# A two-layer diffusion-transformer step on one core: the opening of layer 0 loaded and multiplied in halves of the features, and the first local modulation group moved from steps 3 and 4 to steps 1 and 3

## The reference, cut to what matters

```python
def modulate(cvec, w_mod_l, b_mod_l):
    m = jnp.einsum('bd,de->be', jax.nn.silu(cvec), w_mod_l) + b_mod_l
    return jnp.split(m[:, None, :], N_MOD, axis=-1)

def latent_layer(x, c, ...):
    sh1, sc1, g1, sh2, sc2, g2 = modulate(c, w_mod_l, b_mod_l)
    h = rmsnorm(x, norm1_l) * (1 + sc1) + sh1
    q_mla, ckv, kpe, q_swa, k_swa, v_swa, q_na, k_na, v_na = mixer_projections(h, w_in_l, ...)
    ...
    o_mla = dense_attention(...)
    o_swa = window_attention(...)
    o_na = neighbourhood_attention(..., rpb_l, HEAD_SCALE)
    heads_out = jnp.concatenate([o_mla, o_swa, o_na], axis=-1)
    return residual_tail(x, heads_out, g1, sh2, sc2, g2, ...)
```

## Time and profile before

| What | Value |
|---|---|
| Median of three runs (lowest, highest) | 1337.96 us (1335.44, 1338.13) |
| Profiled execution, its own time | 1338.34 us |
| Its span, first to last instruction | 1336.3 us |
| PE busy / PEld busy | 1279.6 us (96%) / 735.3 us (55%) |
| DVE / ACT / POOL busy | 613.7 / 358.8 / 152.5 us |
| Mean granted TensorE clock | 0.991 of full speed |
| DMA | 313.16 MB, mean 234 GB/s |

### The profile page before, as it was taken

The page is one execution under the profiler, slowest core; times in us unless marked ns, Lnnn a source line. Parts: engine busy times, 40 slices in busy tenths (PEclk is TensorE's granted clock), DMA queues, the critical chain, the costliest instruction groups (busy, mean ns, idle before and its releaser), DMA issues. The chain is left out here.

```text
span 1336.3 us, 17216 instructions
## 1 busy us (share of the span) xinstructions
PE 1279.6 (96%) x6042; PEld 735.3 (55%) x6042; DVE 613.7 (46%) x1519; ACT 358.8 (27%) x931; POOL 152.5 (11%) x257
## 2 busy tenths in 40 slices
PE   6999999999999999999999999989999999999997
PEld 3555555565666564444455555566666656444443
DVE  0132266444566463433343224655556536344438
ACT  1121255434343210000012114563444311100001
POOL 2210220000000110000142003000000011000014
PEclk9999999998999999999999999999899999999999
DMA  9976996499111489999694038430201139999966
GB/s 355 363 248 220 347 332 254 162 359 327 42 64 64 168 333 398 361 374 367 260 334 161 16 140 291 151 128 15 88 33 64 63 130 352 404 368 360 362 270 246
DMA packets 125441, 313.16 MB, mean 234 GB/s; under 512 B 9882, under 2 KB 58426, under 8 KB 112688
## 3 DMA queue, kind: packets, MB, share of 16 engines
q1 hardware_dynamic: 90896, 243.13, 49.8%
q0 software_dynamic: 12848, 45.39, 9.0%
q10 hardware_dynamic: 21616, 23.60, 5.3%
HBM read 232.14 MB, written 80.71 MB: 234 GB/s over the span
## 5 line engine op out<-in xcount | busy, mean ns | idle before, releaser
L790 PE MATMUL ps<-ring,big 128*128 128x384 f32 (+2 forms) x640 | 230.7, 520 | 1.7 <-DVE big L1773 1.3
L790 PEld LDWEIGHTS ps<-ring,big 128*128 128x128 f32 x640 | 120.3, 190 | 104.6 <-issue 63.7
L871 PE MATMUL ps<-ring,arena 128*128 128x512 f32 x384 | 169.3, 594 | 1.9 <-ACT arena L1406 1.9
L502 PEld LDWEIGHTS ps<-consts,arena 128*128 128x128 f32 (+2 forms) x880 | 103.7, 143 | 79.1 <-issue 50.9
L502 PE MATMUL ps<-consts,arena 128*128 128x128 f32 (+2 forms) x880 | 129.7, 278 | 15.7 <-ACT arena L1227 6.6
L711 PE MATMUL ps<-ring,big 128*128 128x512 f32 x320 | 143.0, 598 | 0.8
L563 PE MATMUL ps<-arena 64*128 64x128 f32 (+5 forms) x576 | 137.9, 430 | 6.1 <-DVEq L1822 3.4
L1227 ACT ACTIVATE arena<-ps 128x384 f32<-128x384 f32 (+3 forms) x140 | 69.1, 493 | 221.3 <-PE ps L502 221.3
L871 PEld LDWEIGHTS ps<-ring,arena 128*128 128x128 f32 x384 | 71.2, 190 | 83.1 <-issue 83.1
L563 PEld LDWEIGHTS ps<-arena 64*128 64x128 f32 (+1 forms) x576 | 79.4, 196 | 65.8 <-issue 57.8
L711 PEld LDWEIGHTS ps<-ring,big 128*128 128x128 f32 x320 | 59.0, 190 | 70.4 <-issue 66.4
(11 more groups left out here) (237 smaller groups left out, 1481.9 us busy)
## 6 DMA issues: line engine op xcount, KB each, us to landing
ring<-in_w_mod SPq DMA_DIRECT2D x40, 1024.0 KB, 11.8
ring<-in_w_up SPq DMA_DIRECT2D x22, 1024.0 KB, 9.7
ring<-in_w_gate SPq DMA_DIRECT2D x22, 1024.0 KB, 7.6
slots<-zeros ACTq DMA_DIRECT2D x8, 2560.0 KB, 14.4
slots<-zeros SPq DMA_DIRECT2D x8, 2560.0 KB, 20.2
arena<-in_w_down SPq DMA_DIRECT2D x16, 1024.0 KB, 12.7
arena<-slots SPq DMA_DIRECT2D x30, 512.0 KB, 6.4
slots<-arena POOLq DMA_DIRECT2D x30, 512.0 KB, 9.6
```

Source lines behind the costliest of these rows:

```text
L502: return pe.transpose(out, in_, ident)
L790: mm = pe.matmul(ps[:, c, 0:CHUNKS[c][1]], hT[:, s, k, :], slot[c][:, k, 0:CHUNKS[c][1]], start=(k == 0), stop=(k == KD - 1))
L871: mm = pe.matmul(ps[:, b, :], xgT[:, b, k * P:(k + 1) * P], w_gu[q][:, :, k, :], start=(k == 0), stop=(k == KD - 1))
```

## The change

In the opening of layer 0 the work is cut in two halves a = 0, 1 of the features: each half of the modulation columns (1024 of the 2048: shift and scale of four feature blocks) is loaded with all its rows, then the rows of `w_in` for these feature blocks in all four chunks. PE multiplies modulation half 0, evicts features 0 to 3 of tile 0, and projects tile 0 by features 0 to 3 while half 1 of the modulation is loaded; `first_tile` holds the order. Modulation half 1 is multiplied amid chunk 3 of the first half. The first half's matmuls accumulate in the same banks as the second's. The bias rows of this first group go to `y2` in the arena, which POOL sets to zero before. POOL's vector and cache loads wait for the transposed columns of half 1.

In the local phases of both layers the first modulation group stands in steps 1 and 3, the spins of steps 1 and 3 are gone, its transposes are in step 5 and not 6. The DMA of `rpb` is issued after the eight modulation DMAs and not ahead of them. POOL adds the mask to the bias table in its steps 4 to 7 and not 2 to 5. ACT runs a small Exp before the local phase.

```diff
-MOD_AT = (3, 10, 17)
+MOD_AT = ((1, 3), (10, 11), (17, 18))
...
+            def first_mods(a, ks):
+
+                if ks[0] == 0:
+                    M.take(pe, ("mod", 0, 0, a))
+                pe.wait_ge(mod0_in[2 * a + ks[0] // 4], 32)
+                for k in ks:
+                    for v in range(2):
+                        i = 2 * v + k % 2
+                        mm = pe.matmul(ps[32 * i:32 * i + 32, 7, :], sc[:, k, :], slot0[2 * v + a][:, k, :],
+                                       start=(k < 2), stop=(k >= KD - 2), tile_position=(0, 32 * i))
...
+            def first_tile():
+
+                pe.wait_ge(h_half, 1)
+                for half in range(2):
+                    S[half].take(pe, ("in", 0, 0))
...
+                pe.wait_ge(slot_in[0], 32)
+                part(0, range(0, 4))
+                part(1, range(0, 4))
+                pe.wait_ge(slot_in[1], 32)
+                part(2, range(0, 4))
+                first_mods(1, range(0, 4))
+                first_mods(1, range(4, KD))
+                part(3, range(0, 2))
+                first_columns(1)
+                part(3, range(2, 4))
+                spin(6, 2)
+                pe.wait_ge(T.free, T.freed[("h", 0, 0)])
+                pe.wait_ge(slot_in[2], 32)
+                part(0, range(4, KD))
+                part(1, range(4, KD)).then_inc(S[0].full, 1)
+                turn_entry(0, 1)
+                pe.wait_ge(slot_in[3], 32)
+                part(2, range(4, KD))
+                part(3, range(4, KD)).then_inc(S[1].full, 1)
...
-                        if s == 3:
-                            spin(7, 3)
                         if s < len(pairs):
                             scores(s, (0, 1))
-                        if s < 2:
+                        if s == 0:
                             spin(7, 4)
...
-                sp.wait_ge(T.full, T[("h", L, TILES - 1)])
-                sp.dma_start(bias, t_in["rpb"][L]).then_inc(rpb_in, 16)
                 for half in range(2):
                     sp.wait_ge(S[half].full, S[half][("in", L, TILES - 1)])
                     for part in range(2):
                         mod_load(L, 1, part, (2 * half, 2 * half + 1))
+                sp.dma_start(bias, t_in["rpb"][L]).then_inc(rpb_in, 16)
...
+                act.activation(stat["es"][:, 0:1], mhalf[:, 0:1], ACT.Exp)
                 attention(L, 2)
...
-                    pool.wait_ge(M.full, M[("mc", 0)])
+                    pool.wait_ge(M.full, M[("mc", 0, 1)])
                     vector_loads(0)
...
-                    if 2 <= p < 6:
-                        if p == 2:
+                    if 4 <= p < 8:
+                        if p == 4:
                             pool.wait_ge(rpb_in, 16 * (L + 1))
...
+                    for a in range(2):
+                        first_rows_of(a)
+                        first_columns_of(a)
+                        if a == 0:
+                            h_scale(0, 1)
```

More of the change, by code:

```diff
@@ L509, in mod_group @@
             def mod_group(L, g, ks=range(KD)):
[L511 removed]
                 if ks[0] == 0:
                     M.take(pe, ("mod", L, g))
[L514 to L517 removed]
+                pe.wait_ge(mod_in[ks[0] // 4], 64 * mod_no(L, g))
                 for k in ks:
                     for i in range(4):
[L520 removed]
+                        mm = pe.matmul(ps[32 * i:32 * i + 32, 7, :], sc[:, k, :], slot[i][:, k, :],
                                        start=(k == 0), stop=(k == KD - 1), tile_position=(0, 32 * i))
@@ L523, in mod_group, with first_columns, part @@
                     mm.then_inc(M.full, 1)
-                elif not first:
+                else:
                     mm.then_inc(mod_half, 1)
+            def first_mods(a, ks):
[7 more added lines that the diff above has]
+                                       start=(k < 2), stop=(k >= KD - 2), tile_position=(0, 32 * i))
+                if ks[-1] == KD - 1:
+                    mm.then_inc(M.full, 1)
+            def first_columns(a):
+                M.take(pe, ("mc", 0, a))
+                pe.wait_ge(*((rows_half, 1), (mods_done, 1))[a])
+                for c in range(4):
+                    mm = transpose(ps[:, 7, c * P:(c + 1) * P], y2[:, a, c * P:(c + 1) * P])
+                mm.then_inc(M.full, 1)
+            def first_tile():
+                pe.wait_ge(h_half, 1)
+                for half in range(2):
+                    S[half].take(pe, ("in", 0, 0))
+                def part(c, ks):
+                    for k in ks:
+                        mm = pe.matmul(ps[:, c, 0:CHUNKS[c][1]], hT[:, 0, k, :], slot[c][:, k, 0:CHUNKS[c][1]],
+                                       start=(k == 0), stop=(k == KD - 1), skip_group_check=True)
+                    return mm
+                pe.wait_ge(slot_in[0], 32)
[17 more added lines that the diff above has]
+                part(3, range(4, KD)).then_inc(S[1].full, 1)
             def mod_columns(L):
@@ L736, in _ @@
             pe.wait_ge(sc_set, 3)
-            for quarter in range(4):
-                mod_group(0, 0, range(2 * quarter, 2 * quarter + 2))
-                if quarter == 2:
-                    pe.wait_ge(head_in, 16)
-                    turn_entry(0, 0)
-                if quarter < 3:
-                    spin(3, 6)
-            mod_columns(0)
-            spin(3, 5)
+            first_mods(0, range(0, 4))
+            spin(3, 8)
+            pe.wait_ge(head_in, 16)
+            turn_entry(0, 0)
+            first_mods(0, range(4, KD))
+            first_columns(0)
+            spin(3, 3)
             for L in range(DEPTH):
@@ L1508, in vector_loads @@
                 pool.dma_start(sink[:, :], t_in["swa_sink"][L:L + 1, :].broadcast_to([P, 4])).then_inc(vec_in, 16)
-            for g in range(3):
+            bm = t_in["b_mod"][0].rearrange("(g i n) -> i g n", g=3, i=4)
+            for i in range(4):
+                pool.dma_start(y2[32 * i:32 * i + 2, i % 2:i % 2 + 1, 0:512],
+                               bm[i:i + 1, 0:1].broadcast_to([2, 1, 512])).then_inc(bmod_in, 16)
+            for g in (1, 2):
                 bias_loads(0, g)
@@ L1667, in mod_rows, with first_rows_of, first_columns_of @@
                 dve.sem_inc(M.free, 1)
+            def first_rows_of(a):
+                dve.wait_ge(M.full, M[("mod", 0, 0, a)])
+                if a == 0:
+                    dve.wait_ge(bmod_in, 192)
+                TT(y2[:, a, 0:512], ps[:, 7, :], y2[:, a, 0:512], ALU.add).then_inc((rows_half, mods_done)[a], 1)
+                dve.wait_ge((rows_half, mods_done)[a], 1)
+                dve.sem_inc(M.free, 1)
+            def first_columns_of(a):
+                dve.wait_ge(M.full, M[("mc", 0, a)])
+                dve.wait_ge(head_in, 16)
+                columns = ps[:, 7, :].rearrange("p (c v q r) -> p r v c q", c=4, v=2, q=2)
+                for r in range(2):
+                    last = dve.tensor_reduce(modc[:, r, :, 4 * a:4 * a + 4], columns[:, r], AX.X, ALU.add)
+                then(dve, "dve", last)
+                dve.sem_inc(M.free, 1)
+                scale = modc[:, :, 1, 4 * a:4 * a + 4]
+                STT(scale, scale, 1.0, n1c[:, 0:1, 4 * a:4 * a + 4].broadcast_to([P, 2, 4]), ALU.add,
+                    ALU.mult).then_inc((cols_half, mc_done)[a], 1)
             def mod_columns(L):
@@ L2024, in _ @@
                 if L == 0:
-                    mod_rows(0, 0)
-                    mod_columns(0)
+                    for a in range(2):
+                        first_rows_of(a)
+                        first_columns_of(a)
+                        if a == 0:
+                            h_scale(0, 1)
                 h_evict(L, 0)
```

85 lines of the change are left out of this document (45 added, 40 removed).

## The result

| | before | after |
|---|---|---|
| Median of the runs (lowest, highest) | 1336.74 us (1335.44, 1338.13; 4 runs) | 1351.51 us (1348.43, 1353.84; 4 runs) |
| Ratio, 95% interval | | 1.0109 [1.0084, 1.0133] |
| Profiled execution, its span | 1338.34, 1336.3 us | 1351.66, 1349.5 us |
| Mean granted clock | 0.991 | 0.983 |
| PE / DVE / ACT busy | 1279.6 / 613.7 / 358.8 us | 1276.3 / 616.3 / 359.6 us |

The change costs 14.8 us, against 3.7 predicted, and the time lies above the range. PE is busy for 3.3 us less and the span is 13.2 us longer, so PE waits more and does its work at a lower clock.

A forecast was written before the change was run, and what follows sets the result against it. PE, busy 96% of the span, was taken as the bound. Opening -0.8, layer 0 +3.2, layer 1 -0.4 and clock +1.7 made +3.7 us on 1338.34: middle 1342.0, 8-in-10 range 1335.5 to 1346.0.

The forecast's parts named there:

- The smaller terms: Local phases: uncovered DVE and ACT work after step 4 and POOL's later masks cost 0.5 us in layer 0, 1.0 in layer 1.
- The opening's order: Layer 0's opening: modulation half 1 landing at 38.2, tile 0 ends at 56.6 instead of 57.4, 0.8 us faster.
- The opening's clock: Layer 0's opening: 3.3 us idle before modulation half 1's second part might cost the clock; a bound, 2.1 slower, not summed.
- rival (3): Both idle gaps, 3.3 us in the opening and 4.6 in step 1, cost the clock: 1346.5 us; chance 0.10.
- Layer 0's wait: Local phase, step 1: PE waits 4.6 us for slot 3's first half, pair 2's scores 6.2 later, step 5 2.7 slower.
- Layer 0's clock: Behind step 1's wait the granted clock may fall, slowing 16 matmuls: 0 to 3.3 us, middle 1.7 taken.
- a loss in steps 6 to 9: Sign of being wrong: the local phases lose time in steps 6 to 9; no size given.
- Layer 1: Local phase: weights land earlier, wait under 1 us, step 5 1.4 us faster; 0.4 faster in all after smaller terms.
- MLA: First steps of MLA: their low clock was cited only as evidence on when the clock falls; no term in the sum.
- The table load: ACT's small Exp brings a 1.28 us table load ahead of the first real Exp; counted as gaining nothing.
- Rival (1): Layer 0's wait vanishes because slot 3's first half lands early; the change is faster, 1335.0 us; chance 0.12.
- rival (2): No difference: the wait comes, the clock stays, the opening gives 1 to 2 us more; 1338 to 1340; chance 0.25.

The follow-up runs named there:

- e9: Changed kernel plus four one-matmul zero spins per layer amid MLA's narrow logit-shift matmuls, other waits left open: 1345.24 us, ratio 1.0059 to the kernel before.
- e10: Changed kernel with zero matmuls in the opening's gap (8), layer 0's step 1 (9), both layers' step 3 (3), each MLA (4): 1339.93 us, ratio 1.0019.
- e8: Kernel before plus four one-matmul zero spins per layer amid MLA's narrow logit-shift matmuls: 1334.80 us, ratio 0.9981.
- e1: Kernel before with the new opening alone; local phases, rpb, masks and ACT's Exp as before: 1341.61 us, ratio 1.0031.
- e2: Kernel before with the local change alone (modulation in steps 1 and 3, late rpb and masks, early Exp), old opening: 1346.57 us, ratio 1.006.
- e5: Old opening with the local change, but rpb's load and POOL's mask additions where the kernel before had them: 1344.52 us, ratio 1.0045 to the kernel before.
- e11: Changed kernel with all gaps filled by zero matmuls, and rpb's load and POOL's masks back in steps 2 to 5: 1337.49 us, ratio 1.0006.
- e3: Changed kernel with zero matmuls in its two waits, 8 in the opening and 9 in step 1 of layer 0's local phase: 1344.44 us, ratio 1.0033.
- e6: Kernel before with the new opening and 8 zero matmuls in its gap, local phases as before: 1337.51 us, ratio 1.0000.
- e12: Kernel before with the new opening, 8 spins in its gap, and four spins in MLA of each layer: 1334.38 us, ratio 0.9976.
- e7: Kernel before with the first modulation group in steps 1 and 4, no step 1 spins, loads of features 0 to 3 first: 1341.17 us, ratio 1.0030.
- e4: Kernel before plus one zero spin after every second narrow matmul of MLA's logit shift, eight a layer: 1337.89 us, ratio 1.0002.

## Why the prediction was wrong, by its steps

The sum had -0.8 for the opening, 3.2 and 1.7 for layer 0's local phase, -0.4 for layer 1's, and nothing for MLA: 3.7. By the profiles it was 2.1, 7.1, 0.0 and 3.3, and 0.6 at the end, 13.2 in all. Two steps failed above all. The clock behind the opening's gap was priced at nothing in the sum (2.7 of the 9.5 missing), and the time that MLA spends at the low clock was taken to be the same before and after (3.3). The smaller terms of both layers were too small by 1.4 each, which in layer 1 an earlier step 5 made up for in part, and the clock in layer 0 by 0.7.

The experiments give a ledger of ratios: after 1.0109; its MLA filled 1.0059 (e9); all filled 1.0019 (e10); the kernel before with MLA filled 0.9981 (e8). The loss is thus 6.7 us by the clock in MLA, 5.3 by the clock in opening and local phases, and 5.1 by the order of the work, less the 2.5 that MLA's falls cost the kernel before as well. By the intervals, these have uncertainties of 4, 3, 2 and 2 us. Two of these terms were in the sum, at 1.7 and 2.0; MLA was not.

**The opening's order, predicted -0.8: right.** With the gap filled, the first scores come 0.5 earlier. The landing was 0.75 late (38.95 against 38.2).

**The opening's clock, predicted at nothing: a failed step.** The idle of "3.3 us" was 4.1, and the group behind it 1.7 slower, chunk 3 0.7 slower. With the late landing that turns -0.8 into +2.3; the first scores show +2.1 (in e1, with a shorter fall, +0.7). It stood among the bounds ("2.1 slower") and as rival (3), at 0.10, because the gap was "shorter than the stretch that did it at 298". But a stretch of 3.6 us of narrow matmuls is no bound from below: one observed fall says nothing of the shortest gap that brings one. In e1 3.94 us did it.

**Layer 0's wait, predicted 4.6, and step 5 +2.7: right.** The wait is 4.68. With the clock held, scores of pair 2 are 6.28 late (predicted 6.2) and step 5 2.71 late.

**Layer 0's clock, predicted 1.7 as a middle of 0 and 3.3: mis-sized, 2.4.** Counted from the first scores, scores of pair 2 are 8.70 late in the changed kernel and 6.28 in e10. The 2.4 between them are the slow group, and they stay to the end of the phase. The clock fell in every profile with the wait open: after, e2, e5, e9. The middle of a yes-or-no event was a number that no execution could show; the wait of 4.68 lay above the stretch of the earlier trace rows, and the term should have stood at its full size. The Trainium skill (TensorE: Matmul & The Clock Gate, HAM oscillation) had it: a DMA wait between bursts starts the next burst cold. By that rule, the traces agree, behind both waits.

**The smaller terms, predicted 0.5 and 1.0: mis-sized, 1.9 and 2.4.** In e10 the loss grows from 2.71 at step 5 to 4.58 at step 9 of layer 0, and in layer 1 from -2.41 to -0.05. With masks early (e11) it grows from 2.69 to 3.61 and from -2.31 to -1.51. POOL's additions are 1.0 and 1.6 of it. The rest, 0.9 and 0.8, goes with the modulation group that no longer covers DVE after step 4; what is left after taking masks away was not tested by itself. The prediction had named a loss in steps 6 to 9 as a sign of being wrong.

**Layer 1, predicted -1.4 at step 5 and -0.4 in all.** Step 5 was 2.2 early (2.4 in e10), since no wait came: the half had landed before PE asked. That is not so in every execution: e2, e3 and e5 waited 0.6 to 1.1 us there. And 0.35 of it was gained before, between the first and the second scores, in e1, e6 and e12 as well, which lack the local change, and not in e2 and e5, which lack the new opening. The gain was eaten by the term above.

**MLA, a term put at nothing: the other failed step.** The earlier trace rows showed 13 us at 0.51 in the first steps of MLA, and it was read only as evidence on the clock. It is also a cost that varies from one execution to the next: MLA took 220.3 us with 6.8 us at the low clock and 225.2 with 17.1. In the profiles of the kernels without spins in MLA, these lengths go from 6.8 to 17.1 in either layer. That the changed kernel's profile drew long falls is no single accident: 13.7 of its 43 to 46 us at the low clock lie in the opening and in layer 0, and the 29 to 32 that are left are reached by 13 of the 83 runs of the kernel before, but by all four of the changed one (if the others fell as the profiled one did in those two places, which is not seen). Why they are longer stays open. MLA itself is the same code; the local change alone (e2) had 6.8 in both layers of its profile, the opening alone (e1) 17.1 and 6.8. In size, the 6.7 less the 2.5 is 4.2, with an uncertainty of some 4 us.

**The rest.** The table load gained nothing: from the first scores to the second it is 2.78 us before (161.21 to 163.99) and after (163.34 to 166.12). Rival (1) fell with the landing, rival (2) by the sign. The 0.7 that rival (1) gives layer 0 is not 1.4 less the smaller term of 0.5, which is 0.9; nothing hangs on it. Rival (3) named the mechanism of both waits and priced it at 1346.5; e9, where MLA's falls are taken out, is at 1345.24. With the smaller terms at 1.9 and 2.4 and the 4.2 of MLA it comes to 1346.5 + 1.4 + 1.4 + 4.2 = 1353.5, 2 above the median.

## What to carry to other kernels

When an edit takes spins or cover away, price each new idle stretch of TensorE twice, once as the wait and once as the slow work behind it, and treat the second as an event that happens or doesn't, not as half of it. Cheap filler in a wait that can't be removed gives back the second price: eight spins in the opening and nine in the local phase gave 7 us here. Count the falls elsewhere too, over several executions: here they were as large a term as either wait. And when work is moved, ask what it covered where it stood, and when its weights land: layer 1 lost behind step 5 what it had gained before it, and e7 took a wait out of step 1 and met another in step 4.

## What the runs showed of the hardware

The granted clock falls behind short idle times too, in some executions. In e3, e2 and e9 it fell in step 3 of a local phase, where PE's longest idle time was 1.57 us, before a small score matmul group; in layer 1 of the changed kernel and of e3 the same 1.56 us brought no fall. With three spins there (e10, e11) none fell. The Trainium skill (TensorE: Matmul & The Clock Gate, A second HAM failure mode: psum-queue depth-cycling) tells of a kernel whose clock swings because TensorE is idle for short times between groups of matmuls; e9's row agrees, 5.89 us busy of 7.60 and a clock of 0.78; that it is the same cause is not shown.

Four spins, 1.8 us of work at the 0.46 of e3's row (3.65 for eight), hold the clock in MLA as well as eight; the count of spins in a filler is itself a cost, 3 us between e4 and e8.

DVE's division of two heads takes 0.88 us alone and 1.84 with a POOL addition beside it, a factor of 2.1 for the same instruction in e11 and e10. The Trainium skill (GPSIMD Engine Reference, Specifications) says that GpSimd shares its SBUF interfaces with VectorE, and that it contends with instructions in a perf mode of two ports or with two SBUF inputs. The pair of rows agrees that the two engines contend; the division has one SBUF tensor input, and no row shows its perf mode.
